# Depthwise convolution coefficients on TensorE: diagonals two at a time, in row halves, streamed with the weights

## The reference

```python
def conformer_conv_module(u, w_pw1, b_pw1, dw_w, dw_b, ln_g, ln_b, w_pw2, b_pw2):
    h = u @ w_pw1 + b_pw1
    a, g = jnp.split(h, 2, axis=-1)
    h = a * jax.nn.sigmoid(g)
    h = causal_depthwise_conv(h, dw_w, dw_b)      # 31 coefficients per channel
    h = jax.nn.silu(layernorm(h, ln_g, ln_b))
    return h @ w_pw2 + b_pw2
```

## Time and profile before

| | us |
|---|---|
| median of 3 runs | 2526.17 (2525.43 to 2526.27) |
| the profiled execution | 2526.34 |
| its span, first to last instruction | 2524.5 |
| TensorE busy (matrix products) | 2454.5, 97% |
| VectorE busy | 1252.6, 50% |
| ScalarE busy | 921.2, 36% |
| GpSimd busy | 1041.9, 41% |
| mean granted TensorE clock | 0.986 of full |

### The profile page before, as it was taken

The page is one execution under the profiler, slowest core; times in us unless marked ns, Lnnn a source line. Parts: engine busy times, 40 slices in busy tenths (PEclk is TensorE's granted clock), DMA queues, the critical chain, the costliest instruction groups (busy, mean ns, idle before and its releaser), DMA issues.

```text
span 2524.5 us, 31376 instructions
## 1 busy us (share of the span) xinstructions
PE 2454.5 (97%) x12915; PEld 1990.7 (79%) x12915; DVE 1252.6 (50%) x2020; ACT 921.2 (36%) x1531; POOL 1041.9 (41%) x480
## 2 busy tenths in 40 slices
PE   8999997999999999999999999999999999999999
PEld 6778886888887887788888788887776678788887
DVE  7776667454444797554434632224466545422222
ACT  3434443222223486222223232223567642122221
POOL 4344434544443311744444544443322234544443
PEclk9999998999999999999999999999999999999999
DMA  4112222454442210454432223322211122232322
GB/s 157 50 62 81 71 81 79 160 179 160 154 145 87 88 35 26 150 183 160 165 101 94 88 97 100 96 97 92 68 59 59 51 76 92 84 100 92 100 95 89
DMA packets 70990, 252.69 MB, mean 100 GB/s; under 512 B 8000, under 2 KB 8512, under 8 KB 70848
## 3 DMA queue, kind: packets, MB, share of 16 engines
q1 hardware_dynamic: 58752, 210.27, 25.6%
q10 hardware_dynamic: 12096, 40.42, 4.4%
HBM read 248.56 MB, written 2.10 MB: 99 GB/s over the span
## 4 chain that ended last, share of the span: by engine, by line
PE 87%; DVE 9%; ACT 2%; issue 1%; POOL 0%; ACTq 0%; DMA 0%; DVEq 0%; POOLq 0%
PE ps L510 26%; PE ps L512 26%; PE ps L511 26%; DVE tmpm L1432 1%; DVE arena L1432 1%; PE ps L559 1%; PE ps L552 1%; PE ps L742 1%; PE ps L744 1%; PE ps L743 1%; DVE XL L1441 1%; DVE XL L1432 1%; PE ps L528 1%; PE ps L891 1%; DVE summ L1455 1%
## 5 line engine op out<-in xcount | busy, mean ns | idle before, releaser
L2164 POOL TENSOR_TENSOR WL<-raw,WH 128x1024 fp32r<-128x1024 f32 x391 | 948.7, 2429 | 1225.2 <-ACT WH L930 1218.4
L510 PE MATMUL ps<-XH,WH 128*128 128x512 f32 x3160 | 1251.6, 396 | 39.7 <-DVE XL L1432 15.6
L511 PE MATMUL ps<-XL,WH 128*128 128x512 f32 x3160 | 1240.2, 392 | 0.0
L512 PE MATMUL ps<-XH,WL 128*128 128x512 f32 x3160 | 1239.6, 392 | 0.0
L510 PEld LDWEIGHTS ps<-XH,WH 128*128 128x128 f32 x3160 | 599.4, 190 | 175.9 <-issue 17.7
L511 PEld LDWEIGHTS ps<-XL,WH 128*128 128x128 f32 x3160 | 599.6, 190 | 124.8 <-issue 2.1
L512 PEld LDWEIGHTS ps<-XH,WL 128*128 128x128 f32 x3160 | 598.7, 189 | 125.9
L930 ACT ACTIVATE WH<-raw 128x1024 fp32r<-128x1024 f32 x306 | 322.4, 1057 | 733.8 <-PE ps L512 607.7
L1432 DVE SCALAR_TENSOR_TENSOR arena<-arena,ps 128x512 f32<-128x512 f32 x88 | 60.4, 687 | 516.5 <-ACT arena L1129 505.7
L2162 POOL CAST WH<-raw 128x1024 fp32r<-128x1024 f32 x85 | 93.8, 1104 | 235.8 <-PE ps L512 212.8
L1432 DVE SCALAR_TENSOR_TENSOR h<-ps,der,h 128x512 f32<-128x512 f32 x104 | 77.4, 750 | 160.2 <-PE ps L512 160.1
(11 more groups left out here) (260 smaller groups left out, 1795.0 us busy)
## 6 DMA issues: line engine op xcount, KB each, us to landing
raw<-in_w SPq DMA_DIRECT2D x394, 512.0 KB, 3.3
arena<-in_w_mod ACTq DMA_DIRECT2D x72, 512.0 KB, 3.7
o_out<-h SPq DMA_DIRECT2D x8, 256.0 KB, 2.0
h<-in_x SPq DMA_DIRECT2D x4, 256.0 KB, 7.7
h<-in_x ACTq DMA_DIRECT2D x4, 256.0 KB, 6.6
raw<-in_w SPq DMA_DIRECT2D x2, 256.0 KB, 4.2
arena<-in_c ACTq DMA_DIRECT2D x1, 512.0 KB, 4.3
vec<-in_vec ACTq DMA_DIRECT2D x1, 295.5 KB, 9.8
```

What stands on the lines that cost most here:

```text
L510: e.matmul(b, wh, XH[:, x, :], start=i == 0, stop=False)
L511: e.matmul(b, wh, XL[:, x, :], start=False, stop=False)
L512: p = e.matmul(b, wl, XH[:, x, :], start=False, stop=i == len(slots) - 1)
L2164: e.tensor_tensor(lo, x, hi.bitcast(F32), SUB).then_inc(*did(("split", c)))
```

## The change

- 144 coefficients instead of 92 go to TensorE: 24 of tile 3, 30 of each of tiles 4 to 7. Tiles 0 to 2 stay with VectorE, as do the last coefficients of tiles 3 (7) and 4 to 7 (1).
- One stationary tile holds two coefficients k and k + 1: on its diagonal that of k + 1, and 64 columns aside (modulo 128) that of k. It is used in two row halves, 64 input channels each, which write two banks. In each bank one half of the partitions has the sum of the odd coefficients for these channels, the other half the sum of the even ones, which belongs one token later.
- So a pair of coefficients is six products of 64 x 128 in the order upper half, lower half, upper half and so on.
- The 72 stationary tiles come with the weight stream (nine chunks, 139 to 147). GpSimd casts and splits them, and the first four chunks of the second pointwise products too. The diagonals built by ScalarE and the rounding of the coefficients (L1216, L1876) go.
- For each of tiles 3 to 7 ScalarE copies the even sums, one token later, into the tile's sum (`late_taps`), VectorE adds its own coefficients and then the odd sums and the bias, in two operations of 64 partitions.
- VectorE works through tiles 0 and 1 in turns, then tile 2 alone; tiles 3, 4, 5, 6 and 7 are finished each beside steps of tile 2, as long as there are any.
- The first mean is of tiles 0, 1, 3, 4. Token sums and squares go in the order 0, 1, 3, 4, 5, 2, 6, 7, and the sums stand elsewhere between the coefficients.
- Banks are given by name in this stage; the second pointwise products go round banks 3 to 6 instead of 0 to 4.

```diff
-TAPS = [0, 0, 0, 14, 18, 22, 22, 16]
+TAPS = [0, 0, 0, 24, 30, 30, 30, 30]
...
+    if CHUNK0["taps"] <= c < CHUNK0["p2"] + 4:
+        return False
     return not any(CHUNK0[f] <= c < CHUNK0[f] + 12 for f in ("f0", "f1", "f2", "f3"))
...
+        LN_ORDER = (0, 1, 3, 4, 5, 2, 6, 7)
...
+                        a = {3: 0, 4: 2, 5: 4, 6: 0, 7: 2}[i]
+                        tap_banks[i] = bank(("tap", i, 0), (a,)), bank(("tap", i, 1), (a + 1,))
                     a0 = by_pe.index(i) * W
                     w.wait_ge(*at("xp_lo", i))
+                    for k in range(k0, k1, 2):
+                        wh, wl, c, ends = weights(("taps", 0, i, k))
+                        last = k == TAPS[i] - 2
+                        for n, (d, x) in enumerate(((wh, fh), (wh, fl), (wl, fh))):
+                            for r, b in zip(halves, tap_banks[i]):
+                                p = e.matmul(b, d[r, :], x[r, a0 + k + 1:a0 + k + 1 + T], start=k + n == 0, stop=last and n == 2)
...
+                taps(3, 0, 24)
+                taps(4, 0, 30)
+                taps(5, 0, 10)
+                mean0 = bank(("mean", 0), (6,))
+                mean_of_first(0)
+                taps(5, 10, 20)
+                mean_of_first(1)
+                taps(5, 20, 30)
+                mean_of_first(3)
+                mean_of_first(4)
+                taps(6, 0, 10)
                 w.wait_ge(*at("mean", 0))
+                spread(("mw", 0), small("mean", 0), (6,))
+                taps(6, 10, 30)
+                taps(7, 0, 4)
+                var = bank(("var", 0), (4,))
+                for k, i in enumerate((0, 1, 3, 4)):
                     squares_of(i)
+                    taps(7, 4 + 4 * k, 8 + 4 * k)
+                taps(7, 20, 30)
+                mean = bank(("mean", 1), (5,))
+                for i in LN_ORDER[4:]:
                     mean_of(i)
                     squares_of(i)
...
-                linear([("p2", m) for m in range(4)], [pw2(m) for m in range(4)], list(range(8, 16)), y_at, CB)
+                B2 = (3, 4, 5, 6)
+                linear([("p2", m) for m in range(4)], [pw2(m) for m in range(4)], list(range(8, 16)), y_at, B2)
                 for m in range(4, NT):
-                    linear([("p2", m)], [pw2(m)], list(range(8, 16)), y_at, CB)
+                    linear([("p2", m)], [pw2(m)], list(range(8, 16)), y_at, B2)
...
+                def late_taps(i):
+
+                    w.wait_ge(*at("sum", "tap", i))
+                    A(cv[i][0:64, 1:T], ps("tap", i, 0)[64:128, 0:T - 1], ACT.Copy)
+                    A(cv[i][64:128, 1:T], ps("tap", i, 1)[0:64, 0:T - 1], ACT.Copy).then_inc(*did(("late", i)))
...
+                for i in (3, 4, 5):
+                    late_taps(i)
+                sqrt_table()
+                for i in (0, 1, 3, 4):
                     square(i)
+                late_taps(6)
+                for i in (5, 2, 6):
+                    square(i)
+                late_taps(7)
+                square(7)
...
+                            r = slice(64 * half, 64 * half + 64)
+                            STT(cv[i][r, :], ps("tap", i, half)[r, :], V("dw_b", i)[r, :], cv[i][r, :], ADD, ADD).then_inc(
+                                *did(("free", "tap", i, half), *((("cv", i),) if half else ())))
...
+                more(8)
+                beside(3)
+                beside(4)
+                more(4)
                 w.wait_ge(*at("sum", "mean", 0))
                 v = small("mean", 0)[:, 0:4]
                 TS(v, ps("mean", 0)[:, 0:4], 1.0 / (P * HALF), None, MUL).then_inc(*did(("mean", 0), ("free", "mean", 0)))
+                beside(5)
                 w.wait_ge(*at("sum", "mw", 0))
+                for i in LN_ORDER[:5]:
                     centre(i)
+                more(K)
+                centre(2)
+                for i in (6, 7):
+                    beside(i)
                     centre(i)
```

More of the change, by code:

```diff
@@ L729, in pw1, with taps @@
                     return column("cv_w_pw1", 0, c)
-                def taps(i, k0=0, k1=K):
+                halves = (slice(0, 64), slice(64, 128))
+                def taps(i, k0, k1):
                     if k0 == 0:
-                        tap_bank[i] = bank(("tap", i), CB)
-                    b = tap_bank[i]
+                        a = {3: 0, 4: 2, 5: 4, 6: 0, 7: 2}[i]
+                        tap_banks[i] = bank(("tap", i, 0), (a,)), bank(("tap", i, 1), (a + 1,))
                     a0 = by_pe.index(i) * W
                     w.wait_ge(*at("xp_lo", i))
[L738 to L745, removed]
+                    for k in range(k0, k1, 2):
[4 more added lines that the diff above has]
+                                p = e.matmul(b, d[r, :], x[r, a0 + k + 1:a0 + k + 1 + T], start=k + n == 0, stop=last and n == 2)
+                        if ends or last:
+                            p.then_inc(*did(*([("used", c)] if ends else []), *([("sum", "tap", i)] if last else [])))
                 CB, XB = (0, 1, 2, 3, 4), (5, 6, 7)
-                tap_bank = {}
+                tap_banks = {}
                 linear([("pw", 0, 8), ("pw", 0, 0), ("pw", 0, 9), ("pw", 0, 1)], [pw1(8), pw1(0), pw1(9), pw1(1)], X8, x_at,
@@ L779, in conformer @@
[L779 to L782, removed]
+                    token_sums(var, tmp[LN_ORDER.index(i) % 4], one, i == LN_ORDER[0], i == LN_ORDER[7]).then_inc(
+                        *did(("vs", i), *((("sum", "var", 0),) if i == LN_ORDER[7] else ())))
+                taps(3, 0, 24)
+                taps(4, 0, 30)
+                taps(5, 0, 10)
+                mean0 = bank(("mean", 0), (6,))
@@ L791, in conformer @@
                 w.wait_ge(*at("var"))
-                for n in range(2):
-                    bank(("t", n), XB)
-                spread(("vw", 0), small("var"), CB)
+                bank(("t", 0), (1,))
+                bank(("t", 1), (7,))
+                spread(("vw", 0), small("var"), (2,))
                 def y_at(i):
@@ L1929, in more, with beside @@
                         next(conv, None)
+                def beside(i):
+                    for _ in chains[i]:
+                        more(1)
                 for i in range(NT):
@@ L2195, in layout @@
     w = np.zeros((CHUNKS, P, CT * P), np.float32)
+    lanes = np.arange(P)
     for t, (name, i, rows, cols) in enumerate(stream):
         c, j = divmod(t, CT)
+        if name == "taps":
+            for s in range(2):
+                w[c, lanes, j * P + (lanes + 64 * s) % P] = g["cv_dw_w"][i, cols + 1 - s, rows * P:(rows + 1) * P]
+            continue
         r = 0
```

127 lines of the change are left out of this document (39 added, 88 removed).

## The result

The changed kernel took 2530.62 us (median of 17 runs, 2529.06 to 2533.32), the kernel before 2525.54 in the same comparison (17 runs, 2523.86 to 2526.55): a ratio of 1.0021, 95% interval [1.0014, 1.0029]. It is about 5 us slower. The forecast was 2 us faster; the time lies in the range, but on the other side of no change. The profiled execution took 2529.06 us, span 2527.3, which is the lowest of the 17.

A forecast was written before the change was run, and what follows sets the result against it. The prediction took TensorE as the bound, with VectorE also full in the depthwise stretch. Its terms -8.8 - 0.3 + 5.5 + 1.5 = -2.1 gave 2524.1 us, range 2516.5 to 2532.

The forecast's parts named there:

- The bank wait: Feed-forward's first gate product waits for the residual addition of m = 7, which holds bank 6: +5.5 us.
- Step 1: Coefficient products on TensorE: two half-height products overlap in one slot of 0.24 us, 216 slots replacing 276 products.
- Partial overlap: Rival on the coefficient slots: halves overlap only in part, 0.311 us a slot, +9.2 us, 2535.4; chance 0.10.
- no overlap: Rival on the coefficient slots: halves run one after the other, 0.466 us a slot, 2568.9 us; chance 0.03.
- Step 2: VectorE's list up to tile 4: whole at 934.0, with 3.1 us of GpSimd contention; TensorE waits 4 us.
- Step 3: From tile 4 to the last coefficient product: TensorE sets the pace, ends at 959.5, no clock loss for the wait.
- Step 4: Tail after the last coefficient product: 3.9 us and 0.3 of latency, to 963.7, so -8.8 us; moved cast -0.3.
- The cast's 0.3: ScalarE's cast ahead of the first gate goes to GpSimd, long before: -0.3 us.
- Step 5: Bank order in the second pointwise products: +5.5 us of waiting before the feed-forward, +1.5 for half clock after it.
- The bank wait is short: Rival before the feed-forward: residual chain keeps up with TensorE, only +1.6 us and no clock, 2518.7; chance 0.18.

The follow-up runs named there:

- the fill: Changed kernel with unread products in TensorE's idle places: 14 before tile 4's token sum, 14 before tile 7's, 16 before the second pointwise products; 2527.68 us.
- banks: Changed kernel with the second pointwise products going round banks 6, 3, 4, 5, 0 instead of 3, 4, 5, 6; 2522.96 us.
- later: Changed kernel with ten coefficients of tile 6 put ahead of tile 4's token sum instead of behind it; 2525.47 us.
- PSUM edit: Changed kernel with VectorE's own coefficient of tiles 4 to 7 added in PSUM, before ScalarE's copies rather than behind them; 2530.44 us.
- three-edit kernel: Changed kernel with banks 6, 3, 4, 5, 0, tile 4's sum moved behind ten coefficients, and VectorE's own coefficient in PSUM, no filling products; 2515.30 us.
- two-edit one: Changed kernel with only banks 6, 3, 4, 5, 0 and ten coefficients of tile 6 before tile 4's sum; 2519.48 us.
- repeat: The changed kernel taken again with no edit; 2531.19 us.
- apart: Changed kernel with each pair's three products of one row half listed before the other half's, instead of in turns; 2530.48 us.
- no-subtraction: Changed kernel with GpSimd's subtraction left out for the nine chunks with diagonals; 2526.25 us.
- spread fill: Changed kernel with the three-edit kernel's edits plus 22 filling products: six singly behind sums of tiles 5, 2 and 6, 16 before the second pointwise products; 2518.35 us.

## Why the prediction was wrong, point by point

The forecast was a slight gain, the result a loss of 5 us. The bank wait, the slots and VectorE's lateness at tile 4 were forecast. What failed are steps 3 and 4: half clock behind waits that I had put at nothing or not seen, and one VectorE update held up by GpSimd in the tail.

**Step 1 held.** Slots take 0.232 us, under my 0.24. My estimate of 0.295, carried over from four tiles to two halves with the figure of the Trainium skill (TensorE: Matmul & The Clock Gate, section "Measured speedup vs the span model"), is not borne out. Partial overlap and no overlap both fell.

**Step 2 held in its end and not in its mechanism.** Tile 4's sum starts at 934.02 for a forecast 934.0, but on a line on which the first coefficient product starts 0.99 earlier (897.76 for 898.75), so it is 1 us late and the match of the two numbers is luck. I had taken 0.6 us for each of eight updates scaled by GpSimd's share, 3.1 in all. The trace has two updates of 2.24 and 2.23 (1.5 more each), one of 1.56 and two of 1.01 and 0.90: 4.2 in all. (I had also counted two token sums ahead of tile 4's where the list has three; as VectorE sets the time there, it cost nothing.) The 1.36 us of the earlier trace rows is a partly covered case, which I took for the worst. The worst is the rest of GpSimd's instruction plus 0.55.

**Step 3 missed 1.4 us of clock.** "For the 4 us before tile 6 I take none" is one of the failed choices: of 6.83 us at half clock 3.43 came behind the wait, and the fill there gave 1.4 back. With 1.1 us from step 2, and 90 slots x 0.008 = 0.7 won back from the pitch, this is the 1.8 us by which the stretch fell short (-9.5 for -11.3).

**Step 4 failed most: +6.4 for +2.2** (the tail and the way to p2, 4.9 + 1.5, for 2.5 - 0.3). 2.1 us is the single update beside the subtraction, 2.88 us for the 0.74 I set down: I had applied step 2's contention to tiles 3 and 4 and forgotten that tile 7's last update is of the same form and is on the path. GpSimd is at a chunk of p2 then, whatever the diagonals do. A further 1.5 us is the spreading of the mean, sixteen products in 3.63 us at half clock; the kernel before had them in 2.13. The fill shows that this is the clock: at full clock the way to p2 takes 7.40 us, as before. The cast's 0.3 did not come, and another 0.3 of the tail are small rests.

**Step 5 held, in part by luck.** From p2's first product to the feed-forward's it takes 52.67 us for 47.08: +5.6 for +5.5. The wait is 4.98 us (1028.57 less the last product's 1023.36 and one slot of 0.23) for a forecast 5.1, and that at m = 5 is there, but 0.96 for the 2.4 of the working (1011.15 less 1008.72). I had taken the clock at p2's start as unchanged, since the wait before it is the same 4 us; half clock lasted 6.83 us for 3.41, and m = 4 came 1.35 later. That cost nothing, because the additions of m = 1 to m = 7 are a chain of their own and the wait at m = 5 shrank by as much; the fill showed the same from the other side. With the banks changed it cost nothing either, since the wait for the weights shrank instead: p2 then takes 47.22 us for 47.08. The kernels with banks and later, without and with PSUM, reach m = 4 after 23.74 and 24.64 us and end p2 after 47.21 and 47.28. The half clock behind the wait is 2.2 for 1.5. "The bank wait is short" fell; taking the wait and its clock away brought 7.6 us in the stages.

One thing in this chain is in neither my working nor the experiments. Its pace, 3.6 us in my working, is an average of two. Time line of VectorE in the changed kernel, for the earlier trace rows:

```profile
1011.94 0.74 DVE L1432 SCALAR_TENSOR_TENSOR h<-ps,vec,h 128x512 f32<-128x512 f32 x1
...
1014.75 0.74 DVE L1432 SCALAR_TENSOR_TENSOR h<-ps,vec,h 128x512 f32<-128x512 f32 x1
...
1022.13 1.52 DVE L1455 TENSOR_TENSOR summ<-summ,tmpm 128x512 f32<-128x512 f32 x1
1023.57 0.74 DVE L1432 SCALAR_TENSOR_TENSOR h<-ps,vec,h 128x512 f32<-128x512 f32 x1
...
1027.78 0.74 DVE L1432 SCALAR_TENSOR_TENSOR h<-ps,vec,h 128x512 f32<-128x512 f32 x1
```

The additions of m = 3 and m = 4 are 2.81 us apart, with GpSimd idle; those of m = 6 and m = 7 are 4.21 apart, with GpSimd at casts and subtractions. Between two additions stand two VectorE instructions with both inputs in SBUF, a low part (0.75 us, then 1.31 to 1.67) and a sum of squares (0.68, then 1.52; the one shown ends 0.55 after a cast). At 2.81 us throughout, the addition of m = 7 would follow its own last product, and the feed-forward would start about 4 us sooner; that is an estimate from these rows, and no run shows it.

So the working missed by 1.8 (stretch) + 2.4 (tail) + 1.8 (way to p2) + 0.1 (p2) + 0.7 (clock behind it) = 6.8 us, from -2.1 to +4.8. By cause: clock behind waits 1.4 + 1.5 + 0.7 = 3.6; VectorE shut out by GpSimd 1.1 + 2.1 = 3.2; the cast and small rests 0.7; less 0.7 for the faster slot. Each cause had a row in the trace of before. The earlier trace rows is a wait of 4 us that cost 1.5, and I used that price at one of three new places. The price itself was the smaller of two: ahead of the first pointwise products the kernel before has another such wait, on the time line of TensorE:

```profile
806.44 0.77 PE L510 MATMUL ps<-XH,WH 128*128 128x512 f32 x1 [3.84 <-DVE h L1482]
...
811.69 0.63 PE L510 MATMUL ps<-XH,WH 128*128 128x512 f32 x1
```

The next product starts at 812.12. These 13 steps take 5.68 us, at 0.227 they would take 2.95: a wait of 3.84 us cost 2.7. And on the time line of VectorE in the kernel before stands a full shut-out, ahead of the addition of the earlier trace rows:

```profile
1008.01 2.38 DVE L1432 SCALAR_TENSOR_TENSOR XL<-h,vec,XH 128x512 fp32r<-128x512 f32 x1 [5.83 <-ACT XH L939]
```

It too ends 0.55 us after a GpSimd subtraction (1007.44 and 2.40 us). The same instruction takes 0.75 at 1014.65 and 1.36 at 1024.79. I read these two as "idle" and "at work", and did not ask what a third would show.

What stays open: why half clock lasts 3.41 us in one place and 6.83, 10.24 or 17.07 in others. The runs show only that it starts after or within a stand, and that small shifts of it, as in the PSUM edit, change how much of the following work falls into it. Also open is why the three-edit kernel is 4.2 us under the two-edit one by the medians when the stages give 2.0; the two intervals overlap, so the 2.0 of the stages is the safer figure. And no run leaves out the one GpSimd subtraction beside tile 7's update: that it is the cause there rests on the four other cases, on tile 3 without subtractions, and on the PSUM edit.

## What to carry to other kernels

When work leaves the engine that is full, look for each place where that engine will now stand, and charge each one twice: the wait, and what follows it at half clock. Take off what a later wait for another engine absorbs, as in p2. Then try moving the waiting step behind work that is ready, before making the late engine faster: here one moved sum and one line of banks brought 5.7 and 8.2 us, a faster tail by itself nothing. When GpSimd gets work beside VectorE, charge updates with both inputs in SBUF with the rest of GpSimd's instruction, on the path above all, and give them a PSUM input where that can be had. When banks go round in turns, count through to the first product of the next stage and ask who holds its bank.

## What the runs showed of the hardware that I had not expected

The two row halves of the array start their products in twos whatever the order of the list (0.23 us a two in both orders). VectorE's blocked update ends 0.55 us after GpSimd's instruction ends, although alone it takes 0.74, so a part of it is done already. And TensorE stands for 2.0 to 2.6 us in the tail, marked "issue", each time after 150 records of tiny products in a row (in the changed kernel, its repeat, and the banks, apart, no-subtraction, later and PSUM kernels alike). With single large products in between, a stand of 0.48 us is left, with nothing won by it. What causes it is open. The time line of TensorE in the kernel with the spread fill:

```profile
957.33 0.50 PE L784 MATMUL ps<-XH 128*128 128x512 f32 x1
957.76 0.43 PE L533 MATMUL ps<-cst,tmpm 128*32 128x1 f32 x32
958.13 0.49 PE L784 MATMUL ps<-XH 128*128 128x512 f32 x1
```
